# Norm stages dissolved into their neighbours in a two-block transformer kernel: x turned and split by column group, the root per token applied where sums are evicted

## The reference, cut to what matters

```
h = h + mixer(rms_norm(h, mix_norm[i]))          # i = 0: mixer_a, i = 1: mixer_b
h = h + conv_ffn(rms_norm(h, ffn_norm[i]))
x = rms_norm(h, final_norm)
p = split_columns(rms_norm(x, pre_g[l]) @ w_in + b_in)      # l = 0, 1
x = x + rms_norm(mix(p) @ w_out, post_g[l])
rms_norm(y, g) = y * rsqrt(mean(y * y, over columns) + 1e-6) * g
```

## Time and profile before

| | us |
|---|---|
| median of 3 runs | 3517.47 (3512.8 to 3521.33) |
| the profiled execution's own time | 3513.48 |
| its span, first to last instruction | 3511.5 |
| TensorE busy | 3350.0 (95%), 18952 matmuls |
| VectorE busy | 1944.5 (55%) |
| ScalarE busy | 1621.8 (46%) |
| mean granted TensorE clock | 0.983 of full |

### The profile page before, as it was taken

One profiled execution on the slowest core, in us unless ns is written; L12 is line 12 of the kernel. 1 busy time (PEld: TensorE's weight loads), 2 busy tenths in 40 slices (PEclk: granted clock), 3 DMA queues, 4 the chain that ended last, 5 costly groups with the idle time before them and its releaser, 6 DMA issues. The chain is left out here.

```text
span 3511.5 us, 44784 instructions
## 1 busy us (share of the span) xinstructions
PE 3350.0 (95%) x18952; PEld 2917.5 (83%) x18952; DVE 1944.5 (55%) x2453; ACT 1621.8 (46%) x1850; POOL 0.2 (0%) x4
## 2 busy tenths in 40 slices
PE   7998999999998999999899999999799999899997
PEld 6867888888888897988788888888788887788885
DVE  5665664664654445344566466466555644564644
ACT  5554553553544433343455355344454643354642
POOL 0000000000000000000000000000000000000000
PEclk9999999999999999999999999999899999899998
DMA  5524556556565454544455555555654445654544
GB/s 198 186 88 156 189 190 210 191 190 211 187 207 171 151 180 157 185 153 140 155 188 188 193 189 185 194 185 192 211 177 135 154 162 198 205 180 132 160 157 155
DMA packets 496127, 617.52 MB, mean 176 GB/s; under 512 B 21493, under 2 KB 382975, under 8 KB 494008
## 3 DMA queue, kind: packets, MB, share of 16 engines
q1 hardware_dynamic: 492472, 608.38, 52.6%
q10 hardware_dynamic: 3456, 6.29, 0.5%
HBM read 608.29 MB, written 12.63 MB: 177 GB/s over the span
## 5 line engine op out<-in xcount | busy, mean ns | idle before, releaser
L224 DVE TENSOR_TENSOR low<-raw,high 128x2048 fp32r<-128x2048 f32 (+3 forms) x564 | 1242.7, 2205 | 1104.4 <-ACT high L216 1103.3
L216 ACT ACTIVATE high<-raw 128x2048 fp32r<-128x2048 f32 (+3 forms) x564 | 1039.7, 1845 | 1373.5 <-PE bank L243 736.9
L844 PE MATMUL bank<-h,high 128*128 128x512 f32 x2816 | 993.4, 398 | 6.1 <-PEq L436 6.1
L846 PE MATMUL bank<-h,low 128*128 128x256 f32 x2816 | 791.0, 281 | 0.0
L844 PEld LDWEIGHTS bank<-h,high 128*128 128x128 f32 x2816 | 529.4, 188 | 135.9 <-issue 6.5
L846 PEld LDWEIGHTS bank<-h,low 128*128 128x128 f32 x2816 | 532.7, 189 | 0.2
L241 PE MATMUL bank<-high,y_high 128*128 128x512 f32 x1280 | 499.0, 390 | 8.1 <-PEq L922 5.3
L243 PE MATMUL bank<-high,y_low 128*128 128x512 f32 x1280 | 498.1, 389 | 0.0
L242 PE MATMUL bank<-low,y_high 128*128 128x512 f32 x1280 | 498.1, 389 | 0.0
L1630 PE MATMUL bank<-h,high 128*128 128x512 f32 x1088 | 395.3, 406 | 6.2 <-PEq L436 6.2
L241 PE MATMUL bank<-high,h 128*128 128x256 f32 (+4 forms) x1088 | 352.0, 324 | 6.8 <-PEq L436 6.8
(11 more groups left out here) (236 smaller groups left out, 3091.5 us busy)
## 6 DMA issues: line engine op xcount, KB each, us to landing
raw<-in_w_up SPq DMA_DIRECT2D x176, 1024.0 KB, 5.0
raw<-in_w_down SPq DMA_DIRECT2D x88, 1024.0 KB, 5.1
raw<-in_w_in SPq DMA_DIRECT2D x84, 1024.0 KB, 4.9
raw<-in_b_w_qkv SPq DMA_DIRECT2D x72, 1024.0 KB, 4.9
raw<-in_w_out SPq DMA_DIRECT2D x32, 1024.0 KB, 5.0
raw<-in_a_w_qkv SPq DMA_DIRECT2D x24, 1024.0 KB, 5.0
raw<-in_b_w_o SPq DMA_DIRECT2D x24, 1024.0 KB, 5.1
raw<-in_a_w_o SPq DMA_DIRECT2D x16, 1024.0 KB, 5.1
```

Of the source, the lines that this page charges most:

```text
L216: act.activation(c.high[u % SPLIT][:, 0:n], c.raw[u % RAW][:, 0:n], ACT.Copy).then_inc(c.w_high, 1)
L224: dve.tensor_tensor(c.low[u % RAW][:, 0:n], c.raw[u % RAW][:, 0:n], c.high[u % SPLIT][:, 0:n].bitcast(F32), ALU.subtract).then_inc(c.w_low, 1)
L844: pe.matmul(bank[:, :], wh[:, k, m * P:(m + 1) * P], c.h[:, kt, :, :].rearrange("p a n -> p (a n)"), start=kt == 0, stop=False, skip_group ...
L846: ins = pe.matmul(bank[:, 0:S], wl[:, k, m * P:(m + 1) * P], c.hh[:, kt, :], start=False, stop=kt == 15, skip_group_check=True)
```

## The change

setup_stage, norm_stage, final_norm_stage, the second half's own use of post_stage, and store_stage go. Their work moves into the blocks before and after, by a class Boundary with one object for each of the seven places where x (or the input, or the output) passes from one stage to the next.

- x is not scaled before it is turned. As soon as a column group of x has its last sum, VectorE adds it to x (take); TensorE turns its 8 pieces between two weight units (turn), into the group's own two banks (SUM_BANK); ScalarE makes the high part with the gain (high), VectorE the low part (low), and ScalarE the sums of squares (square, 2 x 128x512 a group). Groups that end too late (late) are done in the first units of the next block (enter_pe, enter_act, enter_dve): group 3 after a mixer, groups 2 and 3 between FFN and mixer B or the hybrid stage, all four between the two hybrid layers (kind "post").
- The factor per token (stats, root) comes during the first units of the next block. Where tokens are in partitions it is the scalar operand of the eviction; where they lie along the free axis a row of 256 factors is made by TensorE (make_row, 2 matmuls) and copied (take_row), and VectorE multiplies by it: in the FFN one more 128x1024 instruction a slab, in b_project evictions (moved from ScalarE to VectorE), in the hybrid stage one more 128x512 instruction for each chan item.
- Between FFN 1 and hybrid layer 0 (kind "final") two norms follow each other: the squares of x, the product with the final gain, then the squares of the product. x itself is scaled later by ScalarE (x_whole), before it is parked.
- The post norm's gain is multiplied in at the eviction of the output groups; squares are taken from the banks; x is updated group by group.
- The input is loaded by column group, between the first weight units, and turned as it arrives. The output is stored in four DMAs of 0.5 MB.
- In FFN slabs the four up units go by halves of K first, so that the first two need chunks 0 to 7 alone. In the hybrid stage the 512-wide tok item comes first, banks 0 to 3 and 4 to 7 change roles, compression starts 4 steps later, parking waits until step 2, w1 loads go from steps 0 and 3 to 3 and 6.

The diff, cut to its core:

```diff
+SUM_BANK = (4, 6, 0, 2)
+class Boundary:
...
+    def take(self, dve, g):
+        dve.wait_ge(c.w_used, self.unit[g] + 1)
+        for t in range(TB):
+            dve.tensor_tensor(self.cols(t, g), self.bank(g, t), self.cols(t, g), ALU.add).then_inc(c.x_taken, 1)
+    def square_early(self, act, g):
+        act.wait_ge(c.x_taken, self.taken0 + 2 * (g + 1))
+        for t in range(TB):
+            act.activation(self.bank(g, t), self.cols(t, g), ACT.Square, accum_out=c.ssq[:, 1, t, g:g + 1]).then_inc(c.x_squared, 1)
+    def scale(self, dve, g):
+        dve.wait_ge(c.x_squared, self.squared0 + self.squares_early(g))
+        for t in range(TB):
+            dve.tensor_tensor(self.cols(t, g), self.cols(t, g), self.fg[g], ALU.mult).then_inc(c.x_scaled, 1)
+    def turn(self, pe, g):
+        if self.kind == "load":
+            pe.wait_ge(c.x_loaded[g], 16)
+        elif self.kind == "final":
+            pe.wait_ge(c.x_scaled, 2 * (g + 1))
+        elif self.kind == "post":
+            pe.wait_ge(c.x_updated, 8 * self.posts() + 2 * (g + 1))
+        else:
+            pe.wait_ge(c.x_taken, self.taken0 + 2 * (g + 1))
...
+        for k in range(4):
+            for t in range(TB):
+                ins = pe.transpose(self.bank(g, k // 2)[:, k % 2 * S + t * P:k % 2 * S + (t + 1) * P],
+                                   c.x[:, t, (4 * g + k) * P:(4 * g + k + 1) * P], c.ident[:, :])
...
+    def await_chunks(self, pe, kt):
+        pe.wait_ge(self.c.h_low, 4 * self.n + kt // 4 + 1)
...
+    def enter_act(self, act, s):
+        if self.kind == "post":
+            if s == 0:
+                self.square_sums(act, 3)
+                self.root_sums(act)
+                self.high(act, 0)
+                self.high(act, 1)
...
+        if s == 1:
+            for g in self.late:
+                self.high(act, g)
+            for g in self.late:
+                self.square(act, g)
+        if s == 2:
+            self.root(act)
+        if s == 3:
+            self.take_row(act)
+            if self.kind == "final":
+                for t in range(TB):
+                    act.activation(c.x[:, t, :], c.x[:, t, :], ACT.Copy, scale=c.stat[:, 5, t:t + 1]).then_inc(c.x_whole, 1)
+    def enter_dve(self, dve, s):
+        if self.kind == "post":
+            if s == 0:
+                self.take_gained(dve, 3)
+                self.invert_sums(dve)
+                self.update(dve, 0)
+                self.update(dve, 1)
+                self.low(dve, 0)
+                self.update(dve, 2)
+                self.low(dve, 1)
+                self.update(dve, 3)
...
 # ffn, ScalarE, VectorE and TensorE
+                        if g0 == 8 and slabs + 1 <= j < slabs + 3: leave.high(act, j - slabs - 1)
+                        elif slabs - 1 <= j < slabs + 1: leave.take(dve, j - slabs + 1)
+                            if g0 == 8 and slabs + 1 <= j < slabs + 3: leave.turn(pe, j - slabs - 1)
-                    dve.tensor_tensor(v[:, par, :, :], c.psum[:, up_banks(n0), 0:S], cv[:, par, :, :], ALU.add).then_inc(summed, 1)
+                    dve.tensor_tensor(v[:, par, :, :], c.psum[:, up_banks(n0), 0:S], cv[:, par, :, :], ALU.add).then_inc(added, 1)
+                    enter.await_row(dve)
+                    dve.wait_ge(added, s0 + n0 + 1)
+                    dve.tensor_tensor(v[:, par, :, :], v[:, par, :, :], c.row[:, :].unsqueeze(1).broadcast_to([P, 4, S]),
+                                      ALU.mult).then_inc(summed, 1)
 # b_project, TensorE and VectorE
+                    if enter and 2 * m + q < 4:
+                        enter.enter_pe(pe, 2 * m + q)
+                    if enter and m == 0:
+                        enter.await_chunks(pe, 8 * q + 7)
+            for j in range(-1, 2 * slabs - 1):
+                if enter and 0 <= j + 1 < 4:
+                    enter.enter_dve(dve, j + 1)
                 split_low(c, dve, u0 + j + AHEAD)
+                if j >= 3 and j % 2:
+                    take(j // 2 - 1)
 # Hybrid, SyncE and VectorE
+            if s == 1:
...
+                if self.enter.kind == "final":
+                    sp.wait_ge(c.x_scaled, 8)
+            if s == 2:
+                if self.enter.kind == "final":
+                    sp.wait_ge(c.x_whole, 2)
+                else:
+                    sp.wait_ge(c.x_updated, 8)
+                sp.dma_start(parked, c.x[:, :, :]).then_inc(self.parked, 16)
...
+        if self.enter.kind == "final":
+            dve.wait_ge(self.final_in, 32)
+        self.enter.enter_dve(dve, 0)
         split_low(c, dve, self.u0 + 1)
...
-            dve.wait_ge(self.halved, 2 * (self.chans.index(n) + 1))
-            dve.scalar_tensor_tensor(out=dst, in0=c.psum[:, bank:bank + 2, 0:S], scalar=self.scale_of(it),
-                                     in1=self.tmp[:, n % 2, :, :], op0=ALU.mult, op1=ALU.add).then_inc(self.taken, 2)
+            dve.tensor_tensor(tmp, c.psum[:, bank:bank + 2, 0:S], tmp, ALU.add).then_inc(self.taken, 2)
+            dve.tensor_tensor(tmp, tmp, c.row[:, :].unsqueeze(1).broadcast_to([P, 2, S]), ALU.mult).then_inc(self.ranked, 1)
 # qkv_product, SyncE
+            load_group(0)
+            load_unit(c, sp, 0)
+            load_group(1)
+            load_unit(c, sp, 1)
+            load_group(2)
+            load_group(3)
+            for u in range(2, RAW):
+                load_unit(c, sp, u)
 # end_stage
+            for g in range(4):
+                sp.wait_ge(c.x_updated, 8 * bound.posts() + 2 * (g + 1))
+                sp.dma_start(rows[:, :, g * 512:(g + 1) * 512], c.x[:, :, g * 512:(g + 1) * 512]).then_inc(stored, 16)
```

More of the change, by code:

```diff
@@ L617, in _ @@
                     split_low(c, dve, u0 + j + AHEAD)
+                if j == 2:
+                    bound.stats(dve)
+                    side.before(chain)
                 side_work(j // per_group - 1, j % per_group - side.wait)
@@ L713, in down_bank @@
         def down_bank(g, t):
-            return c.bank[(4, 0)[g // 2] + 2 * (g % 2) + t]
+            return c.bank[SUM_BANK[g] + t]
+        u0, _, slabs, _ = parts[-1]
+        leave.unit = [u0 + 4 * slabs + final_unit(slabs, g) for g in range(4)]
+        fg = sb("final_gain", [P, D // 2]) if leave.kind == "final" else None
+        fg_loaded = sem("final_gain_loaded") if leave.kind == "final" else None
+        if fg is not None:
+            leave.fg[0], leave.fg[1] = fg[:, 0:512], fg[:, 512:1024]
         @block.sync
@@ L721, in _ @@
                     load_unit(c, sp, u0 + j + RAW)
+                if fg is not None and u0 == parts[0][0]:
+                    broadcast_row(sp, fg[:, :], c.w["final_norm"][0:D // 2], fg_loaded)
         @block.scalar
@@ L1509, in chunk_of, with gains, run @@
         return OUT_ORDER[head // H2] * H2 + head % H2
-    def run(self):
-        c = self.c
+    def gains(self):
+        flat = self.stage[:, :, :].rearrange("p t n -> p (t n)")
+        tmp = self.tmp[:, :, :, :].rearrange("p a b n -> p (a b n)")
+        return [flat[:, 0:512], flat[:, 512:1024], tmp[:, 0:512], tmp[:, 512:1024]]
+    def run(self, layer, enter, leave):
+        c = self.c
+        self.layer, self.enter, self.leave = layer, enter, leave
+        self.u0, self.small = c.u0, c.small[layer]
+        leave.unit = [self.u0 + O0 + j for j in (6, 7, 14, 15)]
+        leave.gp, leave.o = self.gains(), self.o
+        enter.o = self.o
+        if enter.kind == "final":
+            enter.fg[2], enter.fg[3] = self.row[0][:, 0:512], self.row[1][:, 0:512]
```

915 lines of the change are left out of this document (576 added, 339 removed).

## The result

The changed kernel takes 3450.79 us (median of 4 runs, 3446.2 to 3453.19), the kernel before, in the same job, 3516.65 (4 runs, 3512.8 to 3521.33). The ratio is 0.9818 with a 95% interval of 0.9806 to 0.983: 65.9 us or 1.8% faster. Forecast were 3444 us and a gain of 74.

The account below looks back on a forecast made before the run. The prediction took TensorE's stream plus its stops as the bound. Boundary gains less small costs inside stages summed to 74.0 us, from 3513.48 to 3439.5; with the median 4.0 higher it forecast 3444 us, range 3426 to 3472.

Parts of the forecast that it names:

- What bounds the kernel: Whole kernel: TensorE's stream, busy 3350.0 of 3511.5 us, plus its stops; windows around the norms total 154 us.
- Mixer A to FFN 0, mixer B to FFN 1: FFN entries, one group late: 4.9 us in place of 15.33 and of 15.46 + 1.7; gains 10.4 and 12.2.
- FFN 0 to mixer B: Mixer B's entry, two groups late: unit 1 waits 5.4 us; 10.3 against 15.48 + 1.7, gain 6.9 us.
- FFN 1 to hybrid layer 0: Hybrid entry: late final gain load, chain behind it and held SyncE; 16.9 against 25.33 + 1.7, gain 10 us.
- Hybrid layer 0 to 1: Between hybrid layers, all waits for the post norm: 15.3 against 29.85 + 1.7; gain 15.2 after a VectorE allowance.
- FFN windows still all busy: Expected sign in the changed profile: TensorE has no stops inside the FFN windows.
- Start: Kernel start: last input group lands near 14.4, first large matmul at 16.1 us, not 28.81; gain 12.7.
- End: From last matmul to end: four updates, then a 0.5 MB store; 14.5 against 23.86 us, gain 9.4.
- FFN's bound: Rival, FFN slabs: VectorE becomes the bound; at 3 us lost a slab the time is 3576 us; chance 0.05.
- The late groups stalled: Rival, block boundaries: late groups stall TensorE at every one, 24 of 74 us go, 3468 us; chance 0.12.
- Starvation: Rival, hybrid entries: held weight loads cost 20 us at each, gain 34, 3484 us; chance 0.06.
- the case in which four stores are paid in series: Kernel end: each small store pays its fixed part, end gains 3.4 us, not 9.4; 3450 us, chance 0.1.

Follow-up runs that it names:

- ffn_k_inner: Changed kernel with each FFN slab's four up units in the earlier order, halves of K inside, so unit 1 needs the late chunks; 3457.27 us.
- gain_early: Changed kernel with the second half of the final gain loaded during FFN 1, not at hybrid layer 0's start; 3444.6 us.
- park_later: Changed kernel with NSA query jobs at units 8 and 9, x parked at step 5, w1 loaded at steps 2 and 7; 3443.01 us.
- turn_later: Changed kernel with groups 0 and 1 turned, with their high, low and square, one down unit later at FFN 1's end; 3443.52 us.
- start_turns_spread: Changed kernel with input groups 2 and 3 turned after TensorE's first and second weight unit, not before the first; 3462.2 us.
- b_high_first: Changed kernel with ScalarE making the late groups' high parts before its weight split in mixer B's first projection; 3443.21 us.
- the combined version: Changed kernel with turn_later, gain_early, park_later, b_high_first, and the row before unit 4 between FFN 1 and hybrid layer 0; 3426.71 us, ratio 0.9749.

## Why the prediction was right, and where it was not

- *What bounds the kernel* held: TensorE's busy time is the same to 0.6 us, and the gain is standstill taken away. A block end costs 0.99 (forecast 0.9, from the 0.94 of the earlier trace rows). In its reading of the earlier trace rows the prediction gives 0.66 as the lowest clock; the last window there has 0.58. No sum rests on it.
- *Mixer A to FFN 0, mixer B to FFN 1* held. No FFN stood still at its entry; ffn_k_inner shows that the order of the units does it. FFN 0 grew by 2.9 us with its own 24 transposes and the row, in line with the 3.5 for 32 and the 0.5.
- *FFN 0 to mixer B*: the mechanism held, and that 7.3 stands beside 6.9 is luck, since by these windows 8.7 were forecast. The stop is 4.30 where 5.4 with 1.8 of transposes in it, so 3.6, were counted, and the half clock behind it lost 2.3 us (4.5 us of it) in place of 1.7. The split's part was smaller than counted.
- *FFN 1 to hybrid layer 0*: the stops at unit 1 and ahead of the row are where they were forecast, but the sum was too small. The gain is 8.7 where 10.8 were forecast by these windows. The final gain's landing was mis-sized, 7.0 in place of 4.2 us (gain_early: 5.0 us back). The chain behind it was drawn about right: unit 1 began at T+14.6, 7.6 us after the landing, where 8.1 were counted. The held SyncE cost more than twice the 3 us that stood for it, since park_later takes 6.4 back, and mostly as a wait for the parked x, which the forecast did not name. The wait ahead of the row was 1.56 us, where 2.1 were counted.
- *The step that failed* is a term put at nothing without a reason. The prediction has no wait at the end of FFN 1, so groups 0 and 1 cost nothing there but their transposes, and for the kind "final" that was never worked out. I read "FFN windows still all busy" off the plain kind, in which a transpose waits for take alone. In "final" a square on ScalarE and a product on VectorE lie between, in queues that hold a split each. It cost 2.62 + 3.09 of stop and 1.5 for the 3.1 us at half clock behind; turn_later gets 7.6 back.
- *The other part of FFN 1* is no fault of the mechanism. Of its 12.4 us 7.6 are the step above and 2.9 the 24 transposes and the row, as in FFN 0. The remaining 1.9 come from the execution that was profiled before: its FFN 1 had the fast one of two cadences of the same matmuls (explained below; 695 matmuls in 120 us against 681), worth 3.5 us, and lost 1.6 us to half clock at its restart. These are two windows of the kernel before and then one of the changed kernel:

```profile
1733.69:1737.10 3.41, 3.41 (x11) 2.92 (x12) 1.43 (x1) 3.37 (x2) 0.00 (x0) 0.53 0.00 0
1755.00:1875.00 120.00, 120.00 (x695) 105.81 (x694) 78.16 (x78) 63.31 (x59) 0.00 (x0) 1.00 0.57 188
```

```profile
1720.00:1840.00 120.00, 120.00 (x681) 104.14 (x680) 83.70 (x83) 62.77 (x59) 0.00 (x0) 1.00 0.56 184
```

- *Hybrid layer 0 to 1*: 11.67 us and 1.9 in the layer, 2.0 better than forecast. The prediction's sum of 15.3 for this boundary is met; the 2.0 are its two allowances of 1 us for VectorE in the units of layer 1, which were not needed. Nothing shows a stop from the 17 additional multiplications.
- *Start*: mis-sized. First large matmul at 18.45, not 16.1. Group 2 of the input was there at 15.13 (the forecast has 14.4 for the last), and 16 transposes at 3.67 us stood behind it, not 8 at 1.7. They ran at half pace: in start_turns_spread 8 of them take 1.04 us once the matmuls are fast.
- *End*: 13.24 for 14.5. The table load is 1.28 us again, the next instruction right behind it, so the trace still bears out the row and not the 2.66 us of the Trainium skill (ScalarE: Activation LUTs, What ACT_TABLE_LOAD costs).

```profile
3441.06 1.28 ACT L611 ACT_TABLE_LOAD   x1
...
3442.35 0.20 ACT L611 ACTIVATE token_stat<-token_stat 128x2 f32<-128x2 f32 x1
```

- *Rivals.* VectorE did not become FFN's bound: the multiplication by the repeated row takes 1.22 us, as its like, and it would be the bound at 4 to 8 more of them a slab. The late groups stalled where the forecast has them, and at FFN 1's end, and not everywhere. Starvation was there, with 2.55 us and not 20, and hidden behind another wait. That the median, 3450.79, stands beside the 3450 of the case in which four stores are paid in series is chance: the end gained 10.6 us, not 3.4.

## What to carry to other kernels

When a stage is dissolved into in-order queues, write out for every kind of boundary, the last one too, what stands in each engine's list ahead of the awaited instruction; one weight unit more of lead cost nothing here and was worth 7.6 us. A wait in the loader's queue that guards a store belongs where it is already over, since all loads behind it are held. And a stop can cover a second one behind it: after each mend look at the same place again, and move an item on all engines that touch it, not on one.

## What the runs showed of the hardware

**Two cadences of the same matmul stream.** In an FFN's up product at clock 1.00 a pair of matmuls (512 and 256 columns) comes every 353 ns in most stretches and every 346 to 347 in others, for the whole first part of an FFN (32 units). The same program has it in one run and not in another. This is the window from 320 to 440 us of the changed kernel in two runs, with nothing different but the run, each with TensorE busy throughout:

```profile
320.00:440.00 120.00, 120.00 (x681) 104.09 (x680) 82.59 (x82) 62.31 (x59) 0.00 (x0) 1.00 0.57 187
```

```profile
320.00:440.00 120.00, 120.00 (x693) 104.93 (x693) 84.73 (x84) 62.52 (x58) 0.00 (x0) 1.00 0.58 190
```

12 matmuls more in 120 us: FFN 0 took 740.02 us in the one and 737.2 in the other. In all the runs here it is settled by the end of the FFN's first slab and ends with its first part. That makes single times 3 us uncertain for each FFN and is why experiments are read here by windows. What sets it stays open.

**The half clock does not follow a stop's length.** The stop of 4.30 us in mixer B had 6.8 us at a granted clock of 0.50 in one run of the changed kernel, 2.3 of them inside the stop, and 3.4 in the other, all behind the stop. The stop of 3.3 us there had none in b_high_first and 3.4 in the combined version. In attention, 6.8 us follow a stop of 3.25 in the combined version. I would charge 0 to 3.4 us for a stop of this size, and not one value.

**At the very start the clock column says nothing.** The first large matmuls of the changed kernel took 0.78 and 0.63 us, and 0.40 from 20.2 us on, though the windows show a clock of 1.00:

```profile
19.45 0.63 PE L252 MATMUL bank<-high,h 128*128 128x512 f32 x1
...
20.20 0.40 PE L251 MATMUL bank<-low,h 128*128 128x512 f32 x1
```

The trace's first record of the clock is at 20.06 us, and time without a record is counted as 1.00. In start_turns_spread the first record is at 22.20, and the matmuls take 0.63 us until 22. In the kernel before, the same matmul takes 0.63 us where 0.50 is on record (the clock over 28.81 to 34.00 is 0.54):

```profile
29.80 0.63 PE L243 MATMUL bank<-high,h 128*128 128x512 f32 x1
```

So as far as the durations tell these matmuls ran at half clock, as did the transposes ahead of them (8 in 1.97 us, against 1.04 once the matmuls are fast), and a 1.00 for the first 20 us is not to be trusted.
